# First feed-forward network: the second pair of up slabs by seven half-size products

## What is computed

```python
h = x + merged @ w_out[l]
hn = rmsnorm(h, norm_mlp_g[l])
x = h + jnp.square(jax.nn.relu(hn @ w_up[l])) @ w_down[l]     # w_up 1024x4096, w_down 4096x1024
```

## Time and profile before

| | us |
|---|---|
| median of three runs | 1895.57 (1895.26 to 1895.97) |
| the profiled execution | 1895.15 |
| its span, first to last instruction | 1893.4 |
| TensorE busy | 1884.2 |
| VectorE busy | 1172.5 |
| GpSimd busy | 1067.6 |
| ScalarE busy | 762.1 |
| mean granted TensorE clock | 0.999 of 2.4 GHz |

### The profile page before, as it was taken

The page is one execution under the profiler, slowest core; times in us unless marked ns, Lnnn a source line. Parts: engine busy times, 40 slices in busy tenths (PEclk is TensorE's granted clock), DMA queues, the critical chain, the costliest instruction groups (busy, mean ns, idle before and its releaser), DMA issues.

```text
span 1893.4 us, 31153 instructions
## 1 busy us (share of the span) xinstructions
PE 1884.2 (100%) x11449; PEld 1595.8 (84%) x11449; DVE 1172.5 (62%) x2020; ACT 762.1 (40%) x1499; POOL 1067.6 (56%) x1239
## 2 busy tenths in 40 slices
PE   9999999999999999999999999999999999999998
PEld 7788888888888888999898888888888889888887
DVE  7876777767642147677765558788622366565552
ACT  5334433444332245333433545545422443333333
POOL 5454335543445568677766844445564676564645
PEclk9999999999999999999999999999999999999999
DMA  4312221222223432323334322122243223232322
GB/s 161 99 46 89 78 77 31 80 89 69 66 89 100 133 101 89 112 90 101 102 110 138 123 90 78 58 75 68 78 152 104 85 89 105 100 101 93 108 89 89
DMA packets 53467, 176.74 MB, mean 93 GB/s; under 512 B 7744, under 2 KB 8576, under 8 KB 53120
## 3 DMA queue, kind: packets, MB, share of 16 engines
q1 hardware_dynamic: 52880, 172.85, 28.0%
q10 hardware_dynamic: 496, 2.65, 0.4%
HBM read 171.26 MB, written 4.23 MB: 93 GB/s over the span
## 4 chain that ended last, share of the span: by engine, by line
PE 98%; DVE 1%; POOL 0%; DMA 0%; issue 0%; ACT 0%; DVEq 0%
PE bank L321 19%; PE bank L323 19%; PE bank L322 19%; PE bank L909 5%; PE bank L910 5%; PE bank L911 5%; PE bank L861 4%; PE bank L860 4%; PE bank L859 4%; PE bank L2012 2%; PE bank L2006 2%; PE bank L2023 1%; PE bank L2263 1%; PE bank L2250 1%; PE bank L1276 1%; PE bank L1293 1%
## 5 line engine op out<-in xcount | busy, mean ns | idle before, releaser
L310 POOL TENSOR_TENSOR slab_lo<-slab_raw,slab_hi 128x256 fp32r<-128x256 f32 x1156 | 974.4, 877 | 774.1 <-ACT slab_hi L303 774.1
L321 PE MATMUL bank<-u_hi,slab_hi 128*128 128x512 f32 x1176 | 493.1, 419 | 0.2
L323 PE MATMUL bank<-u_hi,slab_lo 128*128 128x512 f32 x1176 | 460.6, 392 | 0.0
L322 PE MATMUL bank<-u_lo,slab_hi 128*128 128x512 f32 x1176 | 459.1, 390 | 0.0
L303 ACT CAST slab_hi<-slab_raw 128x1024 fp32r<-128x1024 f32 (+1 forms) x302 | 301.4, 1011 | 135.0 <-PE bank L911 50.7
L323 PEld LDWEIGHTS bank<-u_hi,slab_lo 128*128 128x128 f32 x1176 | 220.7, 188 | 48.3
L321 PEld LDWEIGHTS bank<-u_hi,slab_hi 128*128 128x128 f32 x1176 | 221.4, 188 | 44.6 <-issue 4.1
L322 PEld LDWEIGHTS bank<-u_lo,slab_hi 128*128 128x128 f32 x1176 | 221.8, 189 | 39.1 <-issue 1.9
L909 PE MATMUL bank<-part_hi,slab_hi 128*128 128x512 f32 x384 | 149.9, 390 | 0.1
L910 PE MATMUL bank<-part_lo,slab_hi 128*128 128x512 f32 x384 | 149.7, 390 | 0.0
L911 PE MATMUL bank<-part_hi,slab_lo 128*128 128x512 f32 x384 | 149.5, 389 | 0.0
(11 more groups left out here) (438 smaller groups left out, 3750.3 us busy)
## 6 DMA issues: line engine op xcount, KB each, us to landing
slab_raw<-slabs SPq DMA_DIRECT2D x302, 512.0 KB, 3.6
g_and_cum_rows<-row_store SPq DMA_DIRECT2D x7, 512.0 KB, 6.2
residual<-x_t SPq DMA_DIRECT2D x4, 512.0 KB, 5.9
residual<-x_t SPq DMA_DIRECT2D x1, 2048.0 KB, 9.1
residual_store<-residual SPq DMA_DIRECT2D x1, 2048.0 KB, 8.8
residual<-residual_store ACTq DMA_DIRECT2D x1, 2048.0 KB, 9.3
out_t<-result_tok SPq DMA_DIRECT2D x4, 256.0 KB, 2.4
out_t<-residual SPq DMA_DIRECT2D x4, 256.0 KB, 2.6
```

The costliest lines, as they stand in the source:

```text
L310: ins = pool.tensor_tensor(w_lo[s][:, ks, :], raw[s][:, ks, :], w_hi[s][:, ks, :].bitcast(F32), ALU.subtract)
L321: pe.matmul(bank, w_hi[s][:, k, :], x_hi[:, k, :], start=first, stop=False)
L322: pe.matmul(bank, w_hi[s][:, k, :], x_lo[:, k, :], start=False, stop=False)
L323: mm = pe.matmul(bank, w_lo[s][:, k, :], x_hi[:, k, :], start=False, stop=last)
```

## The change

The second group becomes fast. The order is now plain, fast, fast, down, fast, down and so on, and there are 15 fast groups in this network instead of 14. The code that each engine ran for the second plain pair goes, and what the first two fast groups need is put in by hand: ScalarE squares slab 1 before the first fast group, and slabs 2 and 3 in the second one, between the copy of product 1 and the next `split_hi`; VectorE makes the split sums of the first group between `lo(0)`, the relu of slab 1 and `lo(1)`. Of slab 3 only the second half is split. No memory is added.

```diff
-MLP_GROUPS = [("plain", 0, 0), ("plain", 0, 2)]
+MLP_GROUPS = [("plain", 0, 0), ("fast", 0, 2)]
...
@@ mlp_pe
-                        t = n + x
-                        if t < 2:
-                            pe.wait_ge(sem("h_new"), KT - 1 + t)
-                        else:
-                            pe.wait_ge(sem("relu"), t - 1)
+                        pe.wait_ge(sem("h_new"), KT - 1 + x)
...
-                            pe.wait_ge(sem("relu"), 3 + x)
+                            pe.wait_ge(sem("relu"), 1 + x)
@@ mlp_act, plain
-                        if n + x == 0:
+                        if x == 0:
                             x_sums_hi(act, 1, 3)
-                        if n + x > 0:
-                            hidden(n + x - 1)
-                        if n + x == 1:
+                        else:
+                            hidden(0)
                             w_sums_hi(act, 0, 0)
                             w_sums_hi(act, 0, 1)
-                    if g == 1:
-                        hidden(n + 1)
+                    hidden(1)
@@ mlp_act, fast
                     f = MLP_FAST.index(g)
+                    if f == 1:
+                        w_sums_hi(act, f, 1)
                     fast_p1_copy(act, f)
+                    if f == 1:
+                        hidden(2)
+                        hidden(3)
                     hi(j + LEAD)
@@ mlp_dve, plain
-                        t = n + x
-                        if t >= 1:
-                            lo(t - 1)
+                        if x == 1:
+                            lo(0)
+                            w_sums_lo(dve, 0, 0)
                         dve.wait_ge(s_used, ph_mlp.index(0, j + x) + 1)
-                        if t >= 2:
-                            dve.wait_ge(sem("hid_sq"), t - 1)
                         relu(rel[x][:], bank_slab[x][:], slice(0, T)).then_inc(sem("relu"), 1)
-                        if t == 0:
+                        if x == 0:
                             w_sums_second(dve, ph_mlp, 2 * MLP_FAST[0], 0)
-                        elif t == 1:
-                            w_sums_lo(dve, 0, 0)
-                        elif t == 2:
-                            w_sums_lo(dve, 0, 1)
-                    if g == 1:
-                        lo(n + 1)
+                    w_sums_lo(dve, 0, 1)
+                    lo(1)
@@ mlp_dve, fast
                     after = f + 1 < len(MLP_FAST)
+                    if f == 1:
+                        w_sums_lo(dve, f, 1)
                     wait_again(dve, "fast_prod", 5 * f + 2)
                     wait_again(dve, "fast_p1", f + 1)
                     post(dve.tensor_tensor(f_v, f_p1, f_2[:, t1], ALU.subtract))
+                    if f == 1:
+                        lo(2)
+                        lo(3)
                     if after:
                         w_sums_first(dve, ph_mlp, 2 * MLP_FAST[f + 1], f + 1)
...
                     post(dve.tensor_tensor(rel[1][:, t1], f_2[:, t1], f_p1, ALU.subtract))
+                    if f == 0:
+                        w_sums_lo(dve, f + 1, 0)
                     wait_again(dve, "fast_post", 6 * f + 5)
```

More of the change, by code:

```diff
@@ L947, in hidden_place @@
         def hidden_place(q):
-            if q < QT:
-                return q % 2, 0, q
-            f, first = divmod(q - QT, 2)
+            if q < 2:
+                return q, 0, q
+            f, first = divmod(q - 2, 2)
             p, n = MLP_GROUPS[MLP_FAST[f]][1:]
@@ L989, in mlp_act @@
                     hi(j + LEAD)
-                    hidden(QT + 2 * f)
+                    hidden(2 + 2 * f)
                     hi(j + LEAD + 1)
-                    hidden(QT + 2 * f + 1)
+                    hidden(2 + 2 * f + 1)
                     if f + 1 < len(MLP_FAST):
@@ L1067, in mlp_dve @@
                     wait_again(dve, "fast_post", 6 * f + 2)
-                    dve.wait_ge(sem("hid_sq"), 2 * f + 3 if f else QT)
+                    dve.wait_ge(sem("hid_sq"), 2 * f + 1 if f else 2)
                     post(dve.tensor_tensor(rel[1][:, t2], f_w, f_3[:, t1], ALU.subtract))
@@ L1072, in mlp_dve @@
                     dve.wait_ge(s_used, ph_mlp.index(0, j) + 1)
-                    dve.wait_ge(sem("hid_sq"), 2 * f + 4 if f else QT - 1)
+                    dve.wait_ge(sem("hid_sq"), 2 * f + 2 if f else 1)
                     post(relu(rel[0][:, t1], f_1[:, t1], t1))
@@ L1087, in mlp_dve @@
                         w_sums_lo(dve, f + 1, 0)
-                    lo(QT + 2 * f)
+                    lo(2 + 2 * f)
                     add(g, p, n)
-                    lo(QT + 2 * f + 1)
+                    lo(2 + 2 * f + 1)
                     add(g, p, n + 1)
```

## The result

| | before | changed |
|---|---|---|
| median of 22 runs each, us | 1895.02 (1894.45 to 1895.97) | 1897.95 (1896.14 to 1898.73) |
| profiled execution, its span | 1895.15, 1893.4 | 1898.3, 1896.5 |

The ratio of the times is 1.0014, 95% interval 1.0008 to 1.0019: slower by 2.9 us in the medians, under the 0.2% that the prediction called no change. The forecast was +1.7 over a kernel before of 1895.57, so 1897.3.

What follows compares the result with a forecast made beforehand. The prediction took TensorE as the bound, busy 1884.2 of 1893.4 us. Its terms, -1.19 + 2.46 + 0 + 0.3 + 0.15 = +1.7 us, moved the median from 1895.57 to 1897.3, range 1896.0 to 1900.1.

Steps and rivals of the forecast that it cites:

- Columns saved and the old wait gone: TensorE, second pair: 84 half-size matmuls replace 48 full ones, gaining 0.80; the wait on slab 0's relu goes, 0.39.
- The gap: TensorE between products 1 and 2 of the new block: waits for the split sums, stall 2.36 plus 0.1 restart.
- The choice between 0.68 and the earlier durations: VectorE's second half of w_sums_second and lo(0): 0.68 each once GpSimd stops, or 1.11 and 1.22, adding up to 0.92.
- Rest of the first block: After product 2 of the new block: product 4 isn't held, 0, at most 0.2 if f_v slips.
- a sign of being wrong: The prediction said it is wrong if product 4 waits in either block.
- Second block: Product 6 waits for f_w, behind lo(2) and lo(3) that wait for ScalarE: +0.3, from 0 to 1.15.
- Down group: Third down product waits for VectorE's addition about 0.55 against 0.41 before: +0.15, bounds -0.1 and +0.25.
- The clock: Rival: clock falls to half in the new stall, 72 matmuls at twice 0.120, 8.6 more, total +10, 1905.9; chance 0.03.
- the other sign of being wrong: The prediction said it is wrong if the clock isn't 1.00 after the gap.
- VectorE throughout: Rival: VectorE bounds both blocks, two-input instructions keep contended durations, product 2 at 734.05; +4.5, 1900.0; chance 0.14.
- Late slab: Rival: slab 9 lands at 748.2, 1.3 after VectorE wants it: +1.3, total +3.0, 1898.6; chance 0.07.
- No wait: Rival: VectorE has the sums ready by 730.8, so only -1.19 is left, 1894.4; chance 0.06.

Runs made afterwards that it cites:

- after_again: The changed kernel run once more with no edit: median 1897.77 us, ratio 1.0012 to the kernel before.
- sums_early: Changed kernel with the sums' second step before the norm's row, their split before slab 0's square, low parts of slabs 0 and 1 behind f_v: 1895.13 us.
- pool_early: early_late_lo with GpSimd making the low part of slab 2 before the norm's power: 1896.14 us, ratio 1.0007 to the kernel before.
- fill18: Changed kernel with 18 unused matmuls of 256 columns between products 1 and 2, filling the gap: 1896.58 us, ratio 1.0008 to the kernel before.
- fill9: Changed kernel with 9 unused matmuls of 256 columns behind product 1, leaving 1.3 us idle: 1896.81 us, ratio 1.0009 to the kernel before.
- early_late_lo: sums_early with the first down group's first addition moved ahead and low parts of slabs 0 and 1 behind the first block's last products: 1895.10 us.
- before_idle_sums: Kernel before with slab 2 also waiting for the first half of the sums' high part, 2.6 us idle: 1897.99 us, ratio 1.0015.
- before_idle_lo: Kernel before with slab 2 also waiting for the low part of slab 0, 3.6 us idle: 1899.36 us, ratio 1.0020.

## Why the prediction was right, and where it wasn't

*Columns saved and the old wait gone, -1.19*: right. In after_again the terms -1.19 + 2.48 + 0.16 + 0.25 + 0.08 give +1.78, measured +1.72.

*The gap, 2.36 + 0.1*: right, 2.37 + 0.10, and for the reason given, as sums_early shows. The choice between 0.68 and the earlier durations was decided as taken: L833 and L1019 take 0.69 each once GpSimd is through (its six pieces take 4.96 us from 725.26). The Trainium skill's rule on the shared access (SBUF — State Buffer, Who interferes with whom) agrees with these rows, and with pool_early's 1.75 against 1.22.

*Rest of the first block, 0 to 0.2*: 0.16 at product 4 when the clock stays up, with f_v ending just before it (735.27 + 0.41 = 735.68 against 735.83); within the term, but the prediction's last paragraph calls a wait at product 4 a sign of being wrong. *Second block, 0.3*: 0.25 then, at product 6 and on f_w, as forecast. But lo(2) and lo(3) ran without waiting for ScalarE (1.28 us together from 745.58): VectorE's own queue set the time. In the changed kernel's first profile it is 0.14; TensorE, slower by 1.5, had given VectorE time (this is argued, not tested). *Down group, +0.15*: +0.08 (0.49 against 0.41).

*The clock*: this step failed, and it is the other sign of being wrong that came. I read one row at the end of the program, where the clock held 4.6 us after the last matmul, and concluded that 2.4 us idle is too short, with a chance of 0.03; and I priced a fall at 8.6, as if it lasted to the end of the block. Both were wrong. The same reading over the 14 profiles of this study gives 2.0 to 5.2 us (2.0 in fill18, 2.6 in fill9, 3.8 in early_late_lo, 4.6 in the kernel before, 5.2 in the changed kernel), so one row was one draw. Nor does the fall have to come while TensorE idles: at 734.1 it came 3.1 us after product 1 and 0.8 us into product 2. When it comes it costs about 1.5 us (profile), not 8.6. Over the runs it costs 1.2 to 1.4 in the median: 1897.95 and 1897.77 against 1896.58 with the gap filled. The Trainium skill (TensorE: Matmul & The Clock Gate, HAM oscillation), whose warning I had set aside on that one row, describes the fall for longer waits than this one; here the runs decide, and a gap of 2.4 us is enough in a large part of them. Of 33 runs of the changed kernel 23 lie above 1897.4, higher than any of the 22 filled ones, and at least 14 of the 33 have a lowered mean clock. What sets the fall off in one run and not in the next stays open.

*The rival "VectorE throughout"*, 1900.0, didn't come: L833 and L1019 were short, and product 4 of the second block did not wait. Its first sign was no good guide: lo(0) ended at 732.10, or 731.92 with the later start of this execution taken off, and the deciding point was 731.9. VectorE and ScalarE were ready for L844 within 0.1 of each other, so there was no room to spare. (The rival's working also leaves out the handover of 0.05: product 2 would have started at 734.10.) *Late slab*: no wait on a landing. *No wait*: a real option, but only with another order on VectorE and ScalarE (sums_early), not in this change.

The time, 1897.95, is 0.65 above the forecast of 1897.3: +1.2 from the clock, -0.55 since the kernel before has a median of 1895.02 over 22 runs instead of 1895.57 over three. That it lies inside the range is in part luck. The range left the clock's case out, and that case came in many of the runs; it fits in because a fall costs a seventh of what I had put on it. (The range's lower end, lower ends of the terms less 0.4, comes to 1896.3 by its own working and not 1896.0; nothing hangs on it.)

## What to carry to other kernels

A saving in matmul columns is worth what is left once the work that was hidden under the removed matmuls has found new cover: here 1.19 us were won and 2.5 exposed, because the sums stood in VectorE's order behind a relu that waits for the norm's row. They don't need the row, and moved ahead of it they left no gap. Count a long exposed gap on TensorE as more than its length (here 2.4 us cost 1.0 to 1.2 more in the median, 1.6 us nothing more), and if it can't be closed, try cheap matmuls in it: they won 1.2 us. Before giving an idle GpSimd work, look what VectorE does in that time: when both read two inputs from SBUF they slow each other (0.42 to 0.84 and 1.22 to 1.75 us on VectorE), and here VectorE was the one on the path.

## What the runs showed of the hardware

After the last matmul of the program the granted clock fell from 1.00 to 0.50 between 2.0 and 5.2 us later, differently from one to the next of 14 executions. How far the median lies above what the stage costs at clock 1.00 depends on the gap: -0.2 us at 1.3 (fill9), 0.0 at 1.6, 1.0 to 1.2 at 2.4 (the changed kernel), 0.9 at 2.6 (before_idle_sums), 1.4 at 3.6 (4.34 against 5.68 - 2.7), where the profiled execution showed the fall. The mean clock was lowered in 0 of 22 runs at 1.3 and 1.6, in 14 of 33 at 2.4, 7 of 11 at 2.6 and 9 of 10 at 3.6, each a lower bound. At 0.50, matmuls of 256 columns start 0.213 apart and those of 512 columns 0.427, against 0.120 and 0.227 at 1.00, so the half clock costs less than double: 0.093 and 0.200 a matmul. It was back at 1.00 after 3.4 us in the changed kernel, and after some 6.8 us in before_idle_lo.
